# Placing, stepping and overlapping the modulation chunks and early loads of a two-network diffusion transformer kernel

## The reference, cut to what matters

```python
mod = (silu(c) @ w_ada[i] + b_ada[i])                 # 6 x 1024 numbers; the same for c_ctx
h   = rmsnorm(x, norm1_w) * (1 + mod[1]) + mod[0]
z   = h @ w_in                                         # 1024 x 3616, then split into q, k, v, gates
x   = x + mod[2] * (mixer(z) @ w_out)                  # GLA (4 heads) and retention (4 heads)
h2  = rmsnorm(x, norm2_w) * (1 + mod[4]) + mod[3]
aff = softmax(h2 @ w_router)                           # 16 experts
gate, idx = top_k(aff.T, 32)                           # each expert picks 32 of 256 tokens
ye  = (silu(h2[idx] @ w_gate) * (h2[idx] @ w_up)) @ w_down * gate
x   = x + mod[5] * scatter_add(ye)                     # w_gate, w_up 1024 x 1408, w_down 1408 x 1024
# then the second network: two layers, with modulation matrices of their own
```

## Time and profile before

| what | us |
| --- | --- |
| median of 3 runs | 1987.08 (1984.13 to 1987.61) |
| the profiled execution, its own time | 1993.03 |
| its span from first to last instruction | 1991.2 |
| TensorE matmul busy | 1753.5 (88%) |
| VectorE busy | 876.7 (44%) |
| ScalarE busy | 552.6 (28%) |
| DMA, mean over the span | 264 GB/s |

### The profile page before, as it was taken

How to read it: one execution, slowest core, us unless ns; L and a number is a source line. 1 busy time by engine, 2 the same in 40 slices (tenths; PEclk the granted TensorE clock), 3 DMA queues, 4 the chain that set the end, 5 groups by cost and what they waited for, 6 DMA issues and landing times.

```text
span 1991.2 us, 30613 instructions
## 1 busy us (share of the span) xinstructions
PE 1753.5 (88%) x13078; PEld 1311.8 (66%) x13078; DVE 876.7 (44%) x1546; ACT 552.6 (28%) x951; POOL 129.1 (6%) x137
## 2 busy tenths in 40 slices
PE   4699898779998988998998897969999989689997
PEld 2579665545554555555555554846899979479997
DVE  0423224232356221111111125874677776966775
ACT  1313413023132010000000003334544443454443
POOL 0000000000000000000000000610000003100000
PEclk8799889779999999999999997989999999799999
DMA  6322795348999999999999996755454513233530
GB/s 269 126 85 85 277 378 211 123 174 367 425 425 424 424 424 425 424 425 424 426 425 424 424 425 249 296 213 191 146 194 169 187 66 128 85 127 128 195 143 21
DMA packets 60165, 526.59 MB, mean 264 GB/s; under 512 B 6410, under 2 KB 9738, under 8 KB 22160
## 3 DMA queue, kind: packets, MB, share of 16 engines
q1 hardware_dynamic: 45888, 471.18, 58.4%
q0 software_dynamic: 14160, 53.70, 6.7%
HBM read 523.80 MB, written 1.05 MB: 264 GB/s over the span
## 4 chain that ended last, share of the span: by engine, by line
PE 59%; DMA 28%; DVE 8%; ACT 2%; POOL 1%; issue 1%; SPq 0%; DVEq 0%; ACTq 0%
PE bank L765 59%; DMA big<-in_w_exp_down 12%; DMA big<-in_w_exp_up 7%; DMA big<-in_w_exp_gate 6%; DVE big L1940 2%; DMA big<-in_w_ada 1%; DVE big L2465 1%; DMA big<-in_ada_w 1%; DVE big L1977 1%; DMA big<-in_ada_half 1%; DVE w_lo L1940 1%; DVE h_lo L1970 1%; DVE big L1963 1%; DMA big<-in_w_in 0%; POOL big L748 0%
## 5 line engine op out<-in xcount | busy, mean ns | idle before, releaser
L765 PE MATMUL bank<-big 128*32 128x352 f32 (+12 forms) x7486 | 1044.0, 428 | 162.3 <-DMA big<-in_w_exp_down 33.9
L765 PEld LDWEIGHTS bank<-big 128*32 128x32 f32 (+5 forms) x7486 | 622.1, 147 | 572.0 <-issue 328.1
L765 PE MATMUL bank<-h_lo,w_hi 128*128 128x256 f32 (+1 forms) x1568 | 453.0, 289 | 0.0
L765 PE MATMUL bank<-h_hi,w_hi 128*128 128x256 f32 x1408 | 407.4, 289 | 33.7 <-DVE h_lo L1970 21.8
L765 PE MATMUL bank<-h_hi,w_lo 128*128 128x256 f32 x1408 | 405.2, 288 | 0.0
L765 PEld LDWEIGHTS bank<-h_lo,w_hi 128*128 128x128 f32 x1568 | 307.8, 196 | 0.7
L765 PEld LDWEIGHTS bank<-h_hi,w_hi 128*128 128x128 f32 x1408 | 275.8, 196 | 44.1 <-issue 29.1
L1940 DVE TENSOR_TENSOR w_lo<-big,w_hi 128x1024 fp32r<-128x1024 f32 x188 | 233.7, 1251 | 149.3 <-ACT w_hi L1913 59.6
L765 PEld LDWEIGHTS bank<-h_hi,w_lo 128*128 128x128 f32 x1408 | 273.7, 194 | 0.7
L1940 DVE TENSOR_TENSOR big<-big 128x256 f32<-128x256 f32 (+6 forms) x201 | 108.5, 546 | 208.9 <-ACT big L1775 147.1
L1913 ACT ACTIVATE w_hi<-big 128x1024 fp32r<-128x1024 f32 x120 | 126.6, 1055 | 97.4 <-PE bank L765 97.4
(11 more groups left out here) (234 smaller groups left out, 1191.4 us busy)
## 6 DMA issues: line engine op xcount, KB each, us to landing
big<-in_w_exp_gate SPq DMA_DIRECT2D x64, 1408.0 KB, 21.7
big<-in_w_exp_up SPq DMA_DIRECT2D x64, 1408.0 KB, 21.7
big<-in_w_exp_down SPq DMA_DIRECT2D x48, 1536.0 KB, 22.7
big<-in_mlp_w SPq DMA_DIRECT2D x32, 2048.0 KB, 7.8
big<-in_w_in SPq DMA_DIRECT2D x17, 2048.0 KB, 8.9
big<-in_u_w POOLq DMA_DIRECT2D x64, 512.0 KB, 9.3
big<-in_w_ada SPq DMA_DIRECT2D x12, 2048.0 KB, 13.5
big<-in_ada_w SPq DMA_DIRECT2D x12, 2048.0 KB, 11.2
```

The costliest lines, as they stand in the source:

```text
L765: return nc.tensor.matmul(o, l, r, start=start, stop=stop)
```

## The change

1. *Early loads.* Chunks are now in a list `ADA` of 24 entries: layer, number, place, PSUM bank. The first four go in the order 0, 2, 1, 3 to slots 1, 2 and to two places behind slot 2 (`early0`, `early1`); the first part of `w_in` goes to slot 0 and is issued third. The sums of squares come after two chunks. The first norm is applied in halves: tiles 0 to 3 after chunks 0 and 2, then the first four weight splits on VectorE, then tiles 4 to 7. ScalarE copies the third chunk's bank after the first half and two weight splits.
2. *Stepping.* The rounds become steps of one or two chunks. A step first does the columns of the chunks that are open (`ada_columns`), then the rows of its own. Chunks 4 to 17 are stepped up to the head norm, 18 and 19 in `w_out`, 20 after the sums of squares, 21 to 23 in the router. Chunks 18 to 23 have two places of their own, `late0` and `late1`; 18 and 19 are issued when the mixer's output is ready, 21 to 23 between the first expert loads.
3. *Projection.* The logarithms move into pairs 5 to 7, the subtraction into pair 8, the decay sums (10 products) behind pair 9. The wait for the gate weights moves from before the projection to the product that reads them.
4. *Retention.* The scores of head n+1 come before the values of head n.
5. *Router.* The transposes to token order move behind the transposes of the affinities, through two banks. ScalarE writes each bank twice, as a high part (`fp32r`) and in full; GpSimd subtracts the low part; `sel` is `fp32r`; the gathering product is 32 `fp32r` products.
6. `w_out`'s products go to banks 4 to 7, and the modulation's bias is added in four calls in place of two.

```diff
+        ADA = [(0, j, b, n % 3) for n, (j, b) in enumerate(((0, "slot1"), (2, "slot2"), (1, "early0"), (3, "early1")))]
+        ADA += [(n // 8, 4 + n if n < 8 else n - 8, f"slot{(1, 0, 2)[n % 3]}", (4 + n) % 3) for n in range(14)]
+        ADA += [(1, 6 + n, ("late0", "late1")[n % 2], n % 2) for n in range(6)]
...
+            ada_load(0)
+            ada_load(1)
+            w_in_load(0)
+            ada_load(2)
+            ada_load(3)
...
+            sp.wait_ge(S("mix1_ready"), 1)
+            ada_load(18)
+            ada_load(19)
+            sp.wait_ge(S("ada_ps"), 19)
+            ada_load(20)
...
+                if n in (2, 4, 5):
+                    late = {2: 21, 4: 22, 5: 23}[n]
+                    sp.wait_ge(S("ada_ps"), late - 1)
+                    ada_load(late)
                 sp.dma_start(dst, src).then_inc(S(f"moe_full{n % 6}"), 16)
...
+            for n in range(4):
+                pool.wait_ge(S("htm_out"), n + 1)
+                tt_, kh = n % 2, n // 2
+                for x in range(2):
+                    i_ = nc.gpsimd.tensor_tensor(htm_lo[tt_ * 4 + 2 * kh + x], htm_full[:, tt_, kh, x * T:(x + 1) * T],
+                                                 htm_hi[:, tt_, kh * 512 + x * T:kh * 512 + (x + 1) * T].bitcast(F32), ALU.subtract)
+                i_.then_inc(S("htm_lo"), 1)
...
+            def ada_step(*chunks):
+
+                ada_columns()
+                for i in chunks:
+                    ada_rows(i)
...
+            for i in range(2):
+                ada_step(i)
+            ada_columns()
             norm_sums(0, N2)
-            ada_first(ADA_FIRST - 1)
+            for i in range(2, ADA_FIRST):
+                ada_step(i)
+            ada_columns()
...
+            ret_scores(0)
+            for hh in range(RH):
+                if hh + 1 < RH:
+                    ret_scores(hh + 1)
+                ret_values(hh)
+            ada_step(16)
...
+            ada_step(23)
+            ada_columns()
 
             pe.wait_ge(S("routed"), 7)
-            pe.wait_ge(S("htm_out"), 4)
             for k in range(KT):
                 if k >= 4:
                     pe.wait_ge(S("xeT_out"), k - 3)
+                if k in (0, 2):
+                    pe.wait_ge(S("htm_out"), k + 2)
+                if k % 4 == 0:
+                    pe.wait_ge(S("htm_lo"), k // 2 + 2)
                 for tt in range(2):
-                    m = mm(PB[k % 4], htm[:, tt, k * P:(k + 1) * P], sel[:, tt, :], tt == 0, tt == 1)
+                    lo = htm_lo[tt * 4 + k // 2][:, k % 2 * P:(k % 2 + 1) * P]
+                    mm(PB[(0, 1, 2, 4)[k % 4]], htm_hi[:, tt, k * P:(k + 1) * P], sel[:, tt, :], tt == 0, False)
+                    m = mm(PB[(0, 1, 2, 4)[k % 4]], lo, sel[:, tt, :], False, tt == 1)
                 m.then_inc(S("xeT_ps"), 1)
...
+            norm_high(0, 0, 4)
+            for u in range(2):
                 w1_high(u)
-            norm_high(0)
+            ada_out(2)
+            for u in range(2, NWB):
+                w1_high(u)
+            ada_out(3)
+            norm_high(0, 4, KT)
...
+            dve.wait_ge(S("rms"), 1)
+            link(V.reciprocal(rs, rs))
+            norm_apply(0, N2, 0, 4)
             for u in range(NWB):
                 w1_low(u)
-            norm_rest(0, N2)
+            modulation(4, [(0, 4, 8), (0, 12, 16)], 7)
+            scales(0, first=4)
+            norm_apply(0, N2, 4, KT)
```

More of the change, by code:

```diff
@@ L376, in build @@
         NWB, WU = 4, KT * P
+        htm_hi = parts32r("htm_hi", B3R["htm"][0], 2, D)
+        sel = parts32r("sel_r", sel_at, 2, E * CAP)
+        htm_lo = [parts32r(f"htm_lo{n}", H_AT + n * N2 + T, T) for n in range(KT)]
         h_hi = [parts32r(f"h_hi{k}", 3 * SLOT + k * N2, N2) for k in range(KT)]
@@ L759, in _ @@
             tiles = Tiles()
-            credit(pe, [f"slot_free{s}" for s in range(3)] + [f"ada_cols{c}" for c in range(3)] + ["h1_ps0", "h1_ps1"])
+            credit(pe, ["h1_ps0", "h1_ps1"])
             for c in range(2):
@@ L768, in take, with ada_rows @@
                 pe.wait_ge(S(f"slot_full{s}"), 16 * (used[s] + 1))
[L770 to L774 removed]
+            early_full = {b: 0 for b in ("early0", "early1", "late0", "late1")}
+            ada_open = []
+            def ada_rows(i):
+                l_, _, b, c = ADA[i]
+                if b.startswith("slot"):
+                    s = int(b[4])
+                    pe.wait_ge(S(f"slot_full{s}"), 16 * (used[s] + 1))
+                    used[s] += 1
+                else:
+                    early_full[b] += 1
+                    pe.wait_ge(S("full_" + b), 16 * early_full[b])
+                if ada_before(i):
+                    pe.wait_ge(S("ada_part"), ada_before(i))
                 for kk in range(2):
@@ L1067, in _ @@
             m.then_inc(S("router_ps"), 1)
+            ada_step(21)
             pe.wait_ge(S("routed"), 3)
@@ L1071, in _ @@
             m.then_inc(S("router_ps"), 1)
+            for n in range(4):
+                if n >= 2:
+                    pe.wait_ge(S("htm_out"), n - 1)
+                for k in range(4):
+                    m = nc.tensor.transpose(PB[(2, 4)[n % 2]][:, k * P:(k + 1) * P],
+                                            h[:, n // 2 * 4 + k, (n % 2) * P:(n % 2 + 1) * P], ident)
+                m.then_inc(S("htm_ps"), 1)
+            ada_step(22)
             pe.wait_ge(S("routed"), 4)
@@ L1546, in _, with norm_high @@
             A(lg[:, 1, :], v0("rdl", 8), ACT.Abs).then_inc(S("log_steps"), 1)
-            def norm_high(k):
+            def norm_high(k, first=0, last=KT):
                 a, _, n = NORMS[k]
                 layer, _, row = NORM_SETS[a]
-                for t in range(KT):
+                for t in range(first, last):
                     act.wait_ge(S("h_scaled"), KT * SPLIT_NORM[k] + t + 1)
@@ L1957, in norm_apply @@
                 hh = h_hi if k else hh1
-                for t in range(KT + 1):
-                    if t < KT:
+                for t in range(first, last_ + 1):
+                    if t < last_:
                         for s_ in range(n // T):
@@ L1987, in _, with modulation @@
                 tt(h[:, t, :], resid[:, t, :], resid[:, t, :], ALU.mult).then_inc(S("sq_d"), 1)
-            def modulation(uses, steps, bank, sets):
-                for c in range(3):
-                    dve.wait_ge(S(f"ada_cols{c}"), uses[c] + 1)
+            def modulation(cols, steps, bank):
+                dve.wait_ge(S("ada_cols"), cols)
                 for layer, first, last in steps:
@@ L2010, in _ @@
             tt(w_sq, v0("norms", 8, KT)[:, 2, :], v0("norms", 8, KT)[:, 2, :], ALU.mult)
-            modulation(ADA_BEFORE, [(0, 0, 4 * ADA_FIRST)], 7, (0,))
+            modulation(2, [(0, 0, 4), (0, 8, 12)], 7)
+            scales(0, last=4)
             def w1_low(u):
@@ L2157, in _ @@
             i_.then_inc(S("mix1_ready"), 1)
-            modulation([ADA_BEFORE[c] + len(ADA_LATER[c::3]) for c in range(3)],
-                       [(0, 4 * ADA_FIRST, 48), (1, 0, 48)], 3, (1, 2, 3))
-            link(tt(asc[:, 2, :, 0:1], asc[:, 2, :, 0:1], v0("norms", 8, KT)[:, 2, :].unsqueeze(2), ALU.mult))
+            scales(1)
             n = PROJ1_END[-1]
```

297 lines of the change are left out of this document (142 added, 155 removed).

## The result

The changed kernel takes **1954.01 us** (median of 4 runs, 1952.86 to 1957.24), the one before in the same runs 1987.34 (1984.13 to 1987.68). The ratio is **0.9838**, with a 95% interval from 0.9821 to 0.9856. It is faster by 33 us by the medians; over all runs on record (50 of the kernel before, 8 of the changed one) the medians are 1990.3 and 1954.7, 36 us apart.

The account below looks back on a forecast made before the run. Weight loads bound the experts, TensorE the stretch after 1210 us, a mixed chain the start; an earlier first expert should pass through. -11.7 + 5.3 - 47 + 2.8 + 3.1 = -47.5 off 1987.1: forecast 1939, range 1925 to 1957.

Parts of the forecast that it names:

- Opening: Start of the kernel: second norm half ends at 61.7 us, against 73.45 for TensorE's last input before, -11.7 us.
- Projection: Projection: ten products moved in cost 4.8 us and VectorE's subtraction is 0.5 late, +5.3 us.
- Mixer stage: From 217.6 to 376.7 us: six chunks and ten products leave, waits shrink, retention heads overlap; -47 us of 159.1.
- waits for VectorE: Mixer stage, retention: with the next head's scores first, heads go from 5.1 to near 3.3 us each, -5 us.
- copy waits: Mixer stage: columns wait no more for a copy at each round's end, 7 x 0.7 = -4.9 us.
- The walk: Mixer stage: walking the new order step by step gives 112 us in place of 159.1, the same as the sum.
- rival (a): Steps run cold: row products at 3.64 instead of 1.92 us, gathering adds 7.5; 1957 us, chance 0.22 shared with rival (c).
- `w_out`: Output product after the mixer stage: one chunk step inside it costs +2.8 us.
- Router: From w_out's last product to the first expert: chunk 23 lands at 34.5 us, gathering follows, 48 us, +3.1.
- Rival (c): Router: GpSimd's parts or chunk 23 come 8 us later and hold the experts; 1947 us, chance 0.22 shared with rival (a).
- rival d: Experts: their 400 us are paced by something that does not start earlier, so no gain passes; 1987 us, chance 0.02.
- rival e: Second network: granted clock falls from 0.93, from 0.865 down eating all 47.5 us; 1999 at 0.85, chance 0.03.

## Why the prediction was right, and where its steps were off

The forecast was 1939, the range 1925 to 1957, the time 1954.0. That is inside the range by 3 us and outside the 1930 to 1948 of the likeliest case. The mechanism was right, the size 14 us too large (-47.5 for -33). About half of that lies in the steps: -47.5 was forecast, the profiled pair gives -40.2. The other half is that the medians are 33 us apart (36 over all runs) and not 40; no step says why.

**Opening (-13.0 for -11.7): right, and for the reasons given.** Five loads in a row, the sums inside them, norm halves, and TensorE idle until ScalarE copies (10.86 us). One part of it gives nothing, the early place of the `w_in` load; the gain came from the places and the halves. The step did name ScalarE's two splits ahead of the copy, but not that putting the copy first costs nothing (4.7 us by the run with the copy first).

**Projection (+6.2 for +5.3): right.** The one wait inside it is VectorE's subtraction, 0.5 us as worked out; the rest is spread over the stage.

**Mixer stage (-41.6 for -47): two terms of the sum failed.** The waits of TensorE in the changed kernel's mixer stage (in total, times, longest):

```profile
PE bank L801 <- DVE big L2002: 12.9, 6, 3.5
PE bank L801 <- DMA big<-in_w_ada: 1.3, 1, 1.3
```

The first products of `w_out` in its order of time:

```profile
328.33 5.92 PE L801 MATMUL bank<-big 128*128 128x256 f32 x13 [3.07 <-DVE big L2002]
```

And its groups of row and column products by form, against the earlier trace rows:

```profile
L801 PE MATMUL bank<-big 128*32 128x512 f32 x224 | 31.5, 700 | 1.8 <-DMA big<-in_w_ada 1.3 <-ACT big L1647 0.5
L801 PE MATMUL bank<-big 128*128 128x2 f32 x136 | 19.4, 273 | 2.6 <-DVE big L2002 2.6
```

| term | forecast | measured | from |
| --- | --- | --- | --- |
| TensorE's busy time: six chunks, decay sums, chunk 16 | -24.2 | -28.4 | 128.16 to 99.75 in the windows; rows and columns alone 72.4 to 50.9 |
| waits for loads, `w_out`'s among them | -13.0 | -13.7 | 15.0 to 1.3 |
| waits for a copy at a round's end | -4.9 | 0 | none in the trace of before |
| waits for VectorE | -5 | +0.5 | 15.5 to 12.9 + 3.1 |
| sum | -47 | -41.6 | |

The **copy waits** were never there. Their price, 0.7 each, was taken from the opening, where a chunk's columns stand alone behind its copy. In the rounds the columns of the chunk before (1.05 us) lie between a chunk's rows and its own columns and cover the copy (0.6 and its handover). The row that says so was at hand: ahead of the 192 column products TensorE waited only for VectorE. The **waits for VectorE**: the heads run at 3.4 us each, near the 3.3 forecast, but the overlap gives 2.9 us (3.6 in the profiled pair) and not 5. The 5.1 us a head of before had been read over a first head at the lower clock (5.14 us for 12 records in the earlier trace rows, 2.83 in each of the next two); without the overlap and at the upper clock it is 4.4. And the order of time shows a wait that did not exist: TensorE stands 3.1 us before `w_out` until VectorE has the mixer's output. In the kernel before, the last round's two chunks stood there and TensorE's work ended at 371.9, when VectorE was done at 372.1; now one chunk stands there. Ahead of the first retention head it is the same: TensorE waited 2.56 us for VectorE behind three chunks, and 4.35 behind two in the run with the heads undone. The forecast took the whole cost of the chunks that leave off, as if they had filled no wait.

How firm is the -41.6? The waits repeat in the second profiles of both kernels, TensorE's busy time does not: with the second profile of the kernel before, the stage's gain would be 48 to 50 us and the forecast of -47 would look met. So the two terms are shown to be wrong by the waits, not by the stage's total.

The walk, which gave the same total and so seemed to confirm the sum, was wrong elsewhere. It held to the tenth of a us at two points of the first third: the second step's second rows 12.7 us after the projection (12.6 forecast), the copy of chunk 10 at 33.4 (rows at 31.5 and 1.9 for them). Then the copy of chunk 12 came at 54.8 instead of about 48.4, because the GLA's values and the products behind them were walked at the upper clock, though the trace of before has 0.57 and 0.50 there. That costs both kernels, so it spoils the walk and not the difference; what it made wrong is the weight of rival (a), whose evidence, the stage's mean clock of 0.81, belonged in part to products that stay. In the mixer stage nothing got dearer by the clock: the mean rose to 0.85.

The Trainium skill ("TensorE: Matmul & The Clock Gate", section "HAM oscillation") tells of the clock falling through waits in which TensorE is idle. The router's rows agree: after 2.63 us of waiting the last rows took 3.64 us, and the granted clock was 0.72 behind them. The mixer's windows do not: 4.00 us busy of 4.00 in four windows and a fall to 0.50, so a rule of waits alone misses this place.

**`w_out` (+2.9 for +2.8): right.**

**Router (+7.5 for +3.1): the place was right, the clock was not.** TensorE waits for `in_ada_w` just before the gathering, as said. Landing 35.2 instead of 34.5 (+0.7), columns 1.87 instead of 1.1 (+0.8), gathering 10.5 instead of 7.5 (+3.0) make up the 4.4 that were missed, within rounding. That is rival (a)'s second half. It was priced at 7.5, for all 32 products at the lower clock; the first 14 ran there. Three kernels with the same router code came out warm, so whether this term is paid is partly luck. Rival (c), the late chunks, did not come 8 us later than forecast, but the forecast's own 34.5 us already held the experts: putting three chunks ahead of three expert loads takes 8 us off where both routers are warm (48.9 to 40.6) and 10 where both are cold (52.5 to 42.4). The step wrote the queue down correctly and did not ask which load is needed first.

**Passing on (rival d) and the second network's clock (rival e): both absent.** 743.2 us from the first expert to the second network's first load, 742.8 before; from the first expert to the end it is 2.3 us less than before, within the spread of that stretch.

So the time came out near rival (a)'s 1957 for the smaller part by its mechanism (the cold gathering, 3 us), for the larger by two waits that the sum had wrong, and for the rest by the unexplained distance of medians and profiles.

## What to carry to other kernels

Take the price of a wait that goes from the waits of its own stage, and ask of work that leaves whether it filled a wait: one of this sum's terms was borrowed from another stage, another took work off whole that had filled waits, and a walk that agreed with them did so by another error. In a queue of large loads ask of each when it is needed: the last chunks, needed before the gathering, stood behind loads needed only after it, and moving them was worth more than the gathering product's new form. Before a single profile of an edit is read for a cause, look whether profiles without the edit show the same: the warm router did. And when an engine's queue holds a short copy that another engine waits for, put it ahead of the long splits.

## What the runs showed of the hardware that was not expected

- TensorE's granted clock can fall to 0.50 while the engine is busy without a gap: four windows of 4.00 us with 4.00 busy at 1.00, 0.57, 0.50, 0.50, in and behind products of 64 columns. The same products halved ran at the upper clock, with 3 us at 0.50 behind them.
- Full float32 products with 512 columns took some 13.7 us for 16 at the upper clock, 32 single-pass products about 7.4. At the lower clock the latter started 0.43 us apart.
- The clock differs between runs of kernels that are alike in a stage: seven profiles with the same router code and chunk 23's landing at 35.2 to 35.4 us gave a router of 52.5 us (four) or 48.9 to 49.0 (three).
